# Issue w2's rows ahead of the w13 pieces of their pair, with three smaller moves, in a two-layer encoder kernel

## What is computed

```python
def swiglu(h, w13, w2):
    a, b = jnp.split(h @ w13, 2, axis=-1)
    return (jax.nn.silu(a) * b) @ w2

for layer in range(DEPTH):
    mod = (cond @ ada_w[layer] + ada_b[layer]).reshape(B_, N_MOD, D)
    sh1, sc1, g1, sh2, sc2, g2, sh3, sc3, g3 = [mod[:, i] for i in range(N_MOD)]
    h = modulate(rmsnorm(x, norm_g[layer, 0]), sh1, sc1)
    x = x + 0.5 * g1[:, None, :] * swiglu(h, ff_w13[layer, 0], ff_w2[layer, 0])
    ...  # mixer, gated by g2
    h = modulate(rmsnorm(x, norm_g[layer, 2]), sh3, sc3)
    x = x + 0.5 * g3[:, None, :] * swiglu(h, ff_w13[layer, 1], ff_w2[layer, 1])
```

## Time and profile before

| | us |
|---|---|
| runs shown: median (lowest to highest) | 935.15 (934.95 to 935.85) |
| profiled execution, its own time | 934.99 |
| its span, first to last instruction | 932.9 |
| TensorE busy | 922.3 (99%) |
| VectorE busy | 709.7 (76%) |
| ScalarE busy | 460.8 (49%) |

### The profile page before, as it was taken

How to read it: one execution, slowest core, us unless ns; L and a number is a source line. 1 busy time by engine, 2 the same in 40 slices (tenths; PEclk the granted TensorE clock), 3 DMA queues, 4 the chain that set the end, 5 groups by cost and what they waited for, 6 DMA issues and landing times.

```text
span 932.9 us, 11280 instructions
## 1 busy us (share of the span) xinstructions
PE 922.3 (99%) x4381; PEld 760.7 (82%) x4381; DVE 709.7 (76%) x715; ACT 460.8 (49%) x643; POOL 111.4 (12%) x177
## 2 busy tenths in 40 slices
PE   9999999999999999999999999999999999999998
PEld 7778788888878888888888888888888888888886
DVE  5886999986979868798887779788767888553544
ACT  4374543445767757343443474452564572443421
POOL 1010112101531100111111001111100110000000
PEclk9999999999999999999999999999999999999999
DMA  9999989977644668999999459986776498565221
GB/s 318 348 376 369 387 295 332 367 249 212 241 146 169 226 204 282 332 317 347 336 310 340 145 185 322 322 286 220 261 255 219 152 339 281 181 199 163 89 91 46
DMA packets 151765, 239.27 MB, mean 256 GB/s; under 512 B 14752, under 2 KB 114848, under 8 KB 151584
## 3 DMA queue, kind: packets, MB, share of 16 engines
q1 hardware_dynamic: 132272, 169.17, 54.6%
q0 software_dynamic: 18864, 69.21, 20.5%
q10 hardware_dynamic: 576, 0.17, 0.1%
HBM read 237.48 MB, written 1.05 MB: 256 GB/s over the span
## 4 chain that ended last, share of the span: by engine, by line
PE 65%; DVE 2%; ACT 1%; issue 1%; POOL 0%; DVEq 0%; POOLq 0%; ACTq 0%
PE ps L1796 42%; PE ps L1993 6%; PE ps L1994 6%; PE ps L1998 6%; PE ps L1958 2%; PE ps L2255 1%; PE ps L1788 1%; PE ps L2008 0%; DVE acc L1256 0%; DVE xn L1343 0%; PE ps L2122 0%; DVE x L1347 0%; PE ps L1915 0%; PE ps L1914 0%; PE ps L1924 0%
## 5 line engine op out<-in xcount | busy, mean ns | idle before, releaser
L1796 PE MATMUL ps<-hi,hT_hi 128*128 128x512 f32 (+1 forms) x788 | 310.7, 394 | 0.8 <-DVE hT_hi L1391 0.8
L1796 PE MATMUL ps<-hi,hT_lo 128*128 128x512 f32 (+1 forms) x788 | 306.0, 388 | 0.0
L1796 PE MATMUL ps<-lo,hT_hi 128*128 128x512 f32 (+1 forms) x772 | 299.2, 388 | 0.0
L1796 PEld LDWEIGHTS ps<-hi,hT_hi 128*128 128x128 f32 x788 | 148.1, 188 | 31.2 <-issue 2.6
L1796 PEld LDWEIGHTS ps<-hi,hT_lo 128*128 128x128 f32 x788 | 148.0, 188 | 30.9 <-DVE hT_lo L1394 0.2
L1193 DVE TENSOR_TENSOR lo<-raw,hi 128x2048 fp32r<-128x2048 f32 (+1 forms) x69 | 155.3, 2256 | 22.3 <-ACT hi L765 22.2
L1796 PEld LDWEIGHTS ps<-lo,hT_hi 128*128 128x128 f32 x772 | 145.2, 188 | 28.7 <-issue 0.2
L765 ACT ACTIVATE hi<-raw 128x2048 fp32r<-128x2048 f32 (+1 forms) x69 | 130.4, 1891 | 9.3 <-DMA raw<-in_ff_w 5.1
L658 POOL DMA_DIRECT2D ada<-in_ada_w x128 | 69.1, 540 | 470.1 <-DVE acc L1256 177.4
L1256 DVE SCALAR_TENSOR_TENSOR acc<-ada,cond,acc 128x1024 f32<-128x1024 f32 x70 | 89.7, 1282 | 9.0 <-DMA ada<-in_ada_w 4.9
L1193 DVE TENSOR_TENSOR lo<-arena,hi 128x2048 fp32r<-128x2048 f32 x29 | 66.4, 2288 | 13.9 <-ACT hi L765 13.9
(11 more groups left out here) (235 smaller groups left out, 1200.0 us busy)
## 6 DMA issues: line engine op xcount, KB each, us to landing
ada<-in_ada_w POOLq DMA_DIRECT2D x128, 512.0 KB, 6.8
raw<-in_ff_w SPq DMA_DIRECT2D x51, 1024.0 KB, 8.0
raw<-in_ff_w SPq DMA_DIRECT2D x96, 512.0 KB, 6.9
arena<-in_ff_w SPq DMA_DIRECT2D x29, 1024.0 KB, 7.8
raw<-in_w_in SPq DMA_DIRECT2D x12, 1024.0 KB, 5.1
ada<-in_ada_w SPq DMA_DIRECT2D x8, 512.0 KB, 8.4
arena<-in_ada_w SPq DMA_DIRECT2D x8, 512.0 KB, 8.8
raw<-in_w_out SPq DMA_DIRECT2D x4, 1024.0 KB, 6.1
```

The lines of the kernel that those rows point to most:

```text
L1796: ins = mm(out, a, b, start=first and m == 0, stop=last and m == len(pairs) - 1, skip_group_check=shared)
```

## The change

Four edits, none of which changes what is computed:

- **SP**: in every pair but the first of each network, `load_w2` for rows 2p+2 and 2p+3 stands ahead of `load_until`. Before, that was so for pair 1 of network 0 alone. In pair 0 of networks 1 to 3 and in pair 10 nothing moves.
- **VectorE, network 0, pairs 3 to 9**: `u_low` stands right behind `w2_low`, ahead of the two ada tiles, and no longer behind them.
- **The first pairs, quarters 2 and 3**: modulated x, from which h's low part is made, is computed by VectorE and no longer by ScalarE. In quarter 1 ScalarE makes h's high part ahead of the second weight unit's.
- **The first pairs, TensorE, quarter 0**: the sum over the columns' partial results (`first_sum(1)`) stands ahead of the second unit's low products and no longer behind them.

```diff
--- before.py
+++ after.py
@@ -597,9 +597,9 @@
                 load_w2(0, q)
             for f in range(4):
                 for p in range(PAIRS):
-                    if (f, p) == (0, 1):
-                        load_w2(0, 4)
-                        load_w2(0, 5)
+                    if p and 2 * p + 2 < NC:
+                        load_w2(f, 2 * p + 2)
+                        load_w2(f, 2 * p + 3)
                     load_until(2 * (FFN_PAIR[f] + p) + 1)
                     if (f, p) == (0, 5):
                         sp.wait_ge(hlo_done, HLO[0] + 16)
@@ -615,7 +615,7 @@
                     if (f, p) == (1, 0):
                         sp.wait_ge(tp_fill, tp_head(3))
                     if 2 * p + 2 < NC:
-                        if f or p > 1:
+                        if f and not p:
                             load_w2(f, 2 * p + 2)
                             load_w2(f, 2 * p + 3)
                     elif f < 3:
@@ -967,12 +967,6 @@
                     j = 2 * q + kk
                     nc.scalar.activation(hT_hi[:, j, :], turned_pair(q, kk), ACT.Identity, bias=modc[:, 0, j:j + 1],
                                          scale=acol[:, 0, j:j + 1]).then_inc(hhi_done, 2)
-            def first_modulated(q):
-
-                for kk in range(2):
-                    j = 2 * q + kk
-                    nc.scalar.activation(x_mod[:, j, :], turned_pair(q, kk), ACT.Identity, bias=modc[:, 0, j:j + 1],
-                                         scale=acol[:, 0, j:j + 1]).then_inc(first_mod, 1)
 
             norm_squares(0, 0)
             norm_squares(0, 1)
@@ -982,11 +976,12 @@
                                      ps[:, TURN_BANK[q], :], ACT.Copy).then_inc(x_copied, 1)
             for q in range(QUARTERS):
                 unit_high(q, 0)
+                if q == 1:
+                    first_high(q)
                 unit_high(q, 1)
-                first_high(q)
+                if q != 1:
+                    first_high(q)
                 unit_high(q, 2)
-                if q > 1:
-                    first_modulated(q)
             w2_high(0)
             w2_high(1)
             silu(0, 0)
@@ -1421,9 +1416,11 @@
                     split_lo(n0 + 2 * p + (2 if p else 3))
                     if p:
                         w2_low(Q0 + 2 * p - 1)
+                    if f == 0 and p:
+                        u_low(f, p - 1)
                     for tile in tiles[2:4]:
                         ada_tile(*tile)
-                    if p:
+                    if f and p:
                         u_low(f, p - 1)
                     if g is not None:
                         mod_half(g, 0, spare_bank(f, p) + 1)
@@ -1535,9 +1532,8 @@
                 if q == 0:
                     first_low(q)
                 unit_low(q, 1)
-                if q == 1:
+                if q:
                     first_modulated(q)
-                if q:
                     first_low(q)
                 if q < QUARTERS - 1:
                     for j in summed_tiles(q + 1):
@@ -1893,8 +1889,11 @@
                     unit_second(q, 0)
                     pe.wait_ge(mod_red, q + 1)
                     first_rows(q + 1, PE_TILES[q + 1])
+                    if q == 0:
+                        first_sum(q + 1)
                     unit_second(q, 1)
-                    first_sum(q + 1)
+                    if q:
+                        first_sum(q + 1)
                     unit_second(q, 2)
                 for i in range(FIRST):
                     unit_high_part(QUARTERS - 1, i)
```

## The result

The changed kernel takes 979.59 us (median of 4 runs, 978.57 to 980.78) against 935.14 us (934.95 to 935.85) for the kernel before on the same chip: a ratio of 1.0472, 95% interval 1.046 to 1.0484. That is 44.5 us slower. The forecast was 966 us, 31 us slower, with a range up to 976: the direction and the places were right, the size was not. The profiled execution has a span of 976.5 us (before 932.9), and its mean granted clock is 0.979 where it was 1.000.

What follows compares the result with a forecast made beforehand. TensorE, busy 922.3 of 932.9 us, bounds the kernel, so its waits count. 934.99 + 33.3 for five stalls - 2.0 for small edits = 966.3, forecast 966 us; range 952 to 976.

Steps and rivals of the forecast that it cites:

- The pairs with four buffers: Pairs 8 to 10 of network 0, 9 and 10 of network 2: late pieces stall TensorE, 33.3 us in all.
- the five turns: SP's turns 7, 8, 9 (network 0) and 8, 9 (network 2): stalls of 7.4, 7.0, 8.1, 3.0, 7.8 us.
- A sixth turn: Network 2, turn of pair 7: pair 9's second piece, asked for only after u's high part, has room; no stall counted.
- The work behind a landing: Network 0, pair 8: after landing, 1.9 us for the high part, then 7.2 us on VectorE to the sum's reduction.
- The landings: Five late pieces: earlier landings of 8.2, 7.9, 6.5, 5.9 and 4.1 us, each plus 1.3 us for the row ahead.
- The sum of the stalls: Five TensorE waits in networks 0 and 2: 7.4 + 7.0 + 8.1 + 3.0 + 7.8 = 33.3 us.
- the last pairs: Pair 10 of networks 0 and 2: TensorE waits for u's parts and before its transposes, 8.1 and 7.8 us.
- stretches of lower granted clock: Sign of being wrong: TensorE's granted clock, 1.00 throughout before, falls behind the stalls.
- The small edits: VectorE, ScalarE and TensorE edits: 1.5 us from u's low part, 0.5 from the first pairs, together -2.0 us (0.7 to 2.8).
- The early rows of w2: ScalarE's 10.06 us wait for a row in pair 3, nearly all covered by TensorE's w13 products: counted as nothing.
- the clock rival: Restarts at low clock after four TensorE stalls over 5 us: +4 us, 970 us, up to 974; chance 0.22.
- the later landings: Bunched pieces queue behind each other and ada, each landing as late as 12 us: 977 us and above; chance 0.08.

Runs made afterwards that it cites:

- the two with zeros: Changed kernel plus products of zeros where TensorE would stand: 975.32 us; with more zeros in pair 9 and the last pairs: 973.86 us.
- the pieces apart: Changed kernel, but in turns 7 and 8 of network 0 SP issues the second piece only when the first has landed: 979.94 us.
- the clock held: Changed kernel with the larger number of zero products filling TensorE's five waits, in pair 9 1.2 us beyond the need: 973.86 us.

## Why the prediction was right in direction and short in size

Two terms of the sum failed: the landings of the two pieces in the middle of network 0 were taken 1.4 and 3.0 us too short, and the fall of TensorE's clock behind the stalls, worth 5.7 us or somewhat more, was left out.

**Where to look: right.** The pairs with four buffers carry the loss: 43 us in the five turns, and nothing in networks 1 and 3. A sixth turn, which had been given room, may have a price of its own: 1.8 us are left open.

**The work behind a landing: right.** 1.9 us for the high part and 7.2 us on VectorE were taken from the earlier trace rows; they measured 1.91 and 7.2.

**The landings: the first mis-sized term.** The forecast took each piece's own landing before plus 1.3 us for the row ahead: 9.5, 9.2, 7.8, 7.2 and 5.4 us. They measured 10.9, 12.2, 7.6, 6.9 and 5.2. (The 8.4 us at 696.99 is the turn of pair 7 of network 2, which was not in the sum.) Three were right within 0.3 us; the two in the middle of network 0 were 1.4 and 3.0 us too short. These two were too short in every execution profiled with SP's new order and the lists as they are, and the other three scatter: in those four (the changed kernel, SP's order alone, and the two with zeros) the five landed after 10.3 to 10.9, 11.2 to 12.8, 7.6 to 8.8, 6.9 to 9.0 and 4.6 to 5.5 us. The forecast added one row, 0.52 MB, to what moves beside a piece; by the packets it was 1.2 and 1.6 MB more in the two that were late (0.9 MB each with the pieces apart). How much each queue counts for stays open.

**The sum of the stalls: right for the wrong reason.** 33.3 us were forecast and 33.4 stood in the trace, but that is a coincidence: pairs 8 and 9 of network 0 were longer than forecast (8.8 and 10.0 against 7.4 and 7.0), and the last pairs shorter (5.9 and 6.0 against 8.1 and 7.8), because TensorE worked through the products between their waits at the low clock, so that part of the time was spent at work. With the clock held the forecast's own quantity is 38.4, without the zeros beyond the need: 5.1 us more than its sum, 2.6 of them in pair 9. The landings account for it: in that execution they exceed the forecast's by 0.8, 2.3, 1.0, 1.2 and -0.1 us, 5.2 together.

**The clock: the second term, left out of the sum.** It stood among the rivals as 4 to 8 us with a chance of 0.22, on the ground that no run had so long a stall. It is shown now: with the clock held the kernel is 5.7 us faster. The prediction itself named stretches of lower granted clock among the signs of being wrong, and they are there (0.50 at 176 to 180 us). The price was about right; the choice was not, since the stalls that the forecast itself counted on were the condition for it. The Trainium skill (TensorE: Matmul & The Clock Gate, HAM oscillation — how this bites in real kernels) names a wait for a transfer as what lowers the clock and adds the price to the waits' time. The first half holds here, in that each stall hangs on a late transfer; the second holds only in part, since 5.7 of 11.8 us were left as time, or 6.9 with the zeros beyond the need.

**The small edits: nearly right in sum.** u's low part gave 1.3 us (1.5 forecast). The first pairs gave nothing (0.5 forecast). The early rows of w2 were counted as nothing, since TensorE's products covered ScalarE's wait for a row; but that wait was behind the same 1.5 us, which are gone with SP's order alone. As both edits remove them, the sum is not touched by this.

**The sum again.** 966.3, plus 5.1 for the landings, plus 5.7 for the clock and 1.2 for the zeros beyond the need, plus 0.5 for the first pairs is 978.8 us; measured are 979.6. The terms come from different executions, so that the last us of agreement may be chance.

**The range.** Its upper end, 976, lies just above the clock rival's 974; the later landings (977 and above) were held a separate case at 0.08. But the two are not exclusive, both came true in part, and by the sum above only together they give 979.

## What to carry to other kernels

An issuing queue that stands strictly in order is a list of waits: moving a transfer that waits for a late event ahead of one that waits for an early one delays the early one by the whole distance, and where few buffers are left that distance ends up on the critical path through whatever stands behind the late data on the other engines. Before counting a late transfer by the work that uses it, read what is queued behind its first use: putting that split last in two lists gave back half of the loss with the transfers issued as late as before. Where a forecast has stalls of several us on TensorE, put the fall of the clock into the sum and not among the rivals, and hold the rivals against each other: those that share a cause add up.

## What the hardware showed that I had not expected

- The clock fell behind the shortest of the five waits too: after 2.70 us of standing it read 0.83, then 0.50 (730 to 734 us), while TensorE was already at work.
- Slow running after a stall is not all loss. TensorE took 11.8 us longer between its stalls, and 5.7 us came back when the clock was held (6.9 with the zeros beyond the need).
- A second 1 MB piece issued 0.7 us behind a first in one queue did not make the first land clearly later: 10.9 and 12.2 us together, 11.0 and 11.6 apart. A piece that is alone lands in 5.7.
